# Mixer projections in three rounded passes, with their branch steps spread over them

## The reference

```python
proj = jnp.einsum("bsd,de->bse", x, w_in)          # 1024 -> 10264 columns
(a_in, gdn_qkv, gdn_beta_in, gdn_decay_in, gdn_gate_in,
 sb_qkv, gla_qkv, gla_lr, gla_gate_in, merge_in) = jnp.split(proj, offsets, axis=-1)
y_a = rg_lru(a_in, ...)                            # causal conv, two gates, scan
qkv = silu(causal_depthwise_conv(gdn_qkv, w))      # then l2-normalised q, k
beta, g = sigmoid(gdn_beta_in), -exp(a_log) * softplus(gdn_decay_in + bias)
y_b = gated_delta_rule(q, k, v, g, beta) ...
y_c = stick_breaking_attention(sb_qkv)
y_d = gla_chunked(gla_qkv, log_sigmoid(gla_lr @ w_gate_up + b) / 16) ...
merged = sum(sigmoid(merge_in[:, :, n]) * (y_n @ w_branch[n]) for n in range(4))
h = merged @ w_out
cos, sin = rope_tables(positions_2, 64)            # used by the second block
```

## Time and profile before

| | |
|---|---|
| median of 3 runs (lowest, highest) | 2191.77 us (2181.67, 2192.86) |
| the profiled execution: its time, its span | 2185.02 us, 2183.2 us |
| mean granted TensorE clock | 0.946 of full |
| busy: PE, DVE, ACT | 2065.7, 1189.5, 903.8 us |

### The profile page before, as it was taken

One profiled execution on the slowest core, in us unless ns is written; L12 is line 12 of the kernel. 1 busy time (PEld: TensorE's weight loads), 2 busy tenths in 40 slices (PEclk: granted clock), 3 DMA queues, 4 the chain that ended last, 5 costly groups with the idle time before them and its releaser, 6 DMA issues.

```text
span 2183.2 us, 29690 instructions
## 1 busy us (share of the span) xinstructions
PE 2065.7 (95%) x12013; PEld 1714.5 (79%) x12013; DVE 1189.5 (54%) x1686; ACT 903.8 (41%) x1300; POOL 60.7 (3%) x144
## 2 busy tenths in 40 slices
PE   8999999989989999998999987999999999879998
PEld 6777778787548888876999962489999999747998
DVE  2060353441269898898655646354565555455544
ACT  1232520211047777675433524443443435464333
POOL 5000000000000000000000000000000000000000
PEclk9999996987979999998999997999999999989999
DMA  7875250302579999996465579455555556403652
GB/s 239 282 262 176 94 174 20 103 14 97 199 323 348 342 351 333 336 350 251 157 198 184 188 307 373 140 173 190 174 194 189 175 173 211 137 25 112 214 189 97
DMA packets 207241, 441.81 MB, mean 202 GB/s; under 512 B 8108, under 2 KB 158732, under 8 KB 183584
## 3 DMA queue, kind: packets, MB, share of 16 engines
q1 hardware_dynamic: 201568, 424.70, 56.0%
q0 software_dynamic: 5568, 15.67, 2.1%
HBM read 439.14 MB, written 1.20 MB: 202 GB/s over the span
## 4 chain that ended last, share of the span: by engine, by line
PE 68%; DVE 6%; ACT 3%; DMA 2%; issue 1%; SPq 0%; ACTq 0%; DVEq 0%
PE P L679 67%; DMA ring<-in_ada_w 1%; ACT merged L1494 1%; DVE w_lo L2032 1%; DVE h L1985 1%; DVE xs L1985 1%; DVE xs L1978 0%; ACT pT L1494 0%; PE P L1206 0%; DMA ring<-in_w_up 0%; DVE w_lo L2427 0%; ACT st L1494 0%; ACT big L1494 0%; DMA ring<-in_w_gate 0%; PE P L1322 0%
## 5 line engine op out<-in xcount | busy, mean ns | idle before, releaser
L679 PE MATMUL P<-x_parts,w_hi 128*128 128x256 f32 x2560 | 458.2, 281 | 2.1 <-DVE w_lo L2032 2.1
L679 PEld LDWEIGHTS P<-x_parts,w_hi 128*128 128x128 f32 x2560 | 399.1, 189 | 8.9 <-DVE w_lo L2032 2.8
L2032 DVE TENSOR_TENSOR w_lo<-ring,w_hi 128x1024 fp32r<-128x1024 f32 x302 | 351.5, 1219 | 80.1 <-ACT w_hi L1526 79.9
L679 PE MATMUL P<-w_hi,x_parts 128*128 128x256 f32 (+2 forms) x1504 | 373.1, 335 | 2.2 <-DVE w_lo L2427 2.2
L679 PE MATMUL P<-x_parts,w_lo 128*128 128x256 f32 x1280 | 361.2, 282 | 0.0
L1526 ACT ACTIVATE w_hi<-ring 128x1024 fp32r<-128x1024 f32 x302 | 297.4, 1050 | 51.4 <-DMA ring<-in_ffn_w_down 48.5
L2427 DVE TENSOR_TENSOR w_lo<-ring,w_hi 128x1024 fp32r<-128x1024 f32 x240 | 281.1, 1221 | 32.5 <-ACT w_hi L1724 29.7
L679 PEld LDWEIGHTS P<-w_hi,x_parts 128*128 128x128 f32 x1504 | 260.9, 193 | 31.1 <-issue 3.3
L1724 ACT ACTIVATE w_hi<-ring 128x1024 fp32r<-128x1024 f32 x240 | 240.6, 1052 | 87.1 <-DMA ring<-in_w_down 31.0
L679 PE MATMUL P<-xT,ring 128*128 128x256 f32 x1152 | 267.4, 389 | 6.9 <-ACT xT L1494 3.1
L679 PEld LDWEIGHTS P<-xT,ring 128*128 128x128 f32 x1152 | 222.5, 195 | 53.6 <-issue 23.1
(11 more groups left out here) (439 smaller groups left out, 2035.8 us busy)
## 6 DMA issues: line engine op xcount, KB each, us to landing
ring<-in_ada_w SPq DMA_DIRECT2D x72, 1024.0 KB, 8.8
ring<-in_ffn_w_gate SPq DMA_DIRECT2D x44, 1024.0 KB, 5.5
ring<-in_ffn_w_up SPq DMA_DIRECT2D x44, 1024.0 KB, 7.9
ring<-in_ffn_w_down SPq DMA_DIRECT2D x44, 1024.0 KB, 4.9
ring<-in_w_in SPq DMA_DIRECT2D x40, 1024.0 KB, 7.4
ring<-in_w_gate SPq DMA_DIRECT2D x40, 1024.0 KB, 5.0
ring<-in_w_up SPq DMA_DIRECT2D x40, 1024.0 KB, 5.0
ring<-in_w_down SPq DMA_DIRECT2D x40, 1024.0 KB, 5.2
```

Of the source, the lines that this page charges most:

```text
L679: return pe.matmul(o, l, r, start=start, stop=stop, **kw)
L2032: dve.tensor_tensor(w_lo[:, slot, c:c + half], ring[:, slot, c:c + half], w_hi[:, slot, c:c + half].bitcast(F32), ALU.subtract).then_inc(s ...
```

## The change

P2 to P23 run in three float32r passes. `x` gets a high and a low part (`xm_hi`, over the place of `xs`, and `xm_lo`); the weights' high parts go to `wm_hi`, two units deep, over the place of `rowbc`. ACT's and DVE's halves of a unit's split are a step `split`, p, two units ahead: it stands behind P(p-2) (p = 3: behind `cols`) and ahead of the branch steps put there. `xs` is loaded a second time by POOL, after the last projection. The small products are one group of 40 rows in three passes, behind P2; a step `beta` transposes the 8 beta and decay rows back, behind P3. The `b_conv` and `a_conv` steps are cut into tiles and spread over P4 to P15, `a_mult` is cut in two, `b_silu` comes in three pieces. `b_norm` stands behind P18 (before: P19), `c_z` 0 behind P21 (before: P22). The 20 `ada` units stand behind P2 to P17. The `angles` and the sine go to merges 24 and 29. `x` is loaded in two halves at the start, ACT loads its table for the copies ahead of them, and the first two merges wait each for its own bank. The semaphores of the a, b and d branches are shared (`branch_act`, `branch_dve`), with the same waits.

```diff
     STEPS[k:k] = steps
 
 
-_put(("proj", "a", 1), [("cols",), ("small",), ("a_conv",)])
-_put(("proj", "b", 3), [("angles",)])
-_put(("proj", "b", 7), [("a_gates",)])
-_put(("proj", "c", 0), [("a_mult",)])
-_put(("proj", "c", 1), [("a_scan",)])
-_put(("proj", "c", 5), [("b_conv",)])
-_put(("proj", "d", 3), [("b_norm",)])
+PROJ = list(STEPS)
+WHOLE = 2
+
+
+_put(PROJ[1], [("cols",)])
+_put(PROJ[2], [("small",)])
+_put(PROJ[3], [("beta",)])
+_put(PROJ[4], [("a_conv", 0)])
+_put(PROJ[5], [("a_conv", 1), ("b_conv", 0)])
+_put(PROJ[6], [("b_conv", 1), ("b_conv", 2)])
+_put(PROJ[7], [("b_conv", 3), ("b_conv", 4)])
+_put(PROJ[8], [("b_conv", 5), ("b_conv", 6), ("b_silu", 0)])
+_put(PROJ[9], [("b_conv", 7), ("a_gates",)])
+_put(PROJ[10], [("b_conv", 8), ("b_silu", 1)])
+_put(PROJ[11], [("a_mult", 0)])
+_put(PROJ[12], [("a_mult", 1)])
+_put(PROJ[13], [("b_conv", 9), ("b_conv", 10)])
+_put(PROJ[14], [("a_scan",)])
+_put(PROJ[15], [("b_conv", 11)])
+_put(PROJ[16], [("b_silu", 2)])
+_put(PROJ[18], [("b_norm",)])
+for p in range(WHOLE, len(PROJ)):
+    _put(("cols",) if p == 3 else PROJ[p - 2], [("split", p)])
 for n in reversed(range(EARLY_ADA)):
-    _put([s for s in STEPS if s[0] == "proj"][2 + n * 17 // EARLY_ADA], [("ada", n)])
...
+_put(("split", 23), [("c_z", 0)])
 STEPS.append(_MERGE[0])
...
 
...
         w_lo = buf("w_lo", 128, R, UNIT, dt=F32R, ctx=m0)
         m0.close()
         ring = buf("ring", 128, R, UNIT)
+        m0 = ExitStack()
+        xm_hi = buf("xm_hi", 128, DT, S, dt=F32R, ctx=m0)
+        buf("xT_place", 128, DT, S, ctx=m0)
+        wm_hi = buf("wm_hi", 128, 2, UNIT, dt=F32R, ctx=m0)
+        m0.close()
         xs = buf("xs", 128, 2, D)
         m0 = ExitStack()
...
-            sp.dma_start(xs[:, :, :], A["x"][0].rearrange("(i p) d -> p i d", p=128)).then_inc(sem("x_here"), 16)
+            for i in range(2):
+                sp.dma_start(xs[:, i, :], A["x"][0][i * 128:i * 128 + 128, :]).then_inc(sem("x_rest" if i else "x_here"), 16)
             passed, after_unit = Counter(), []
             for n in range(len(loads)):
...
             store_quad(1, 0)
+            pool.wait_ge(sem("proj_out"), 2 * len(PROJ))
+            load(xs[:, :, :], A["x"][0].rearrange("(i p) d -> p i d", p=128), "ln_here")
             pool.wait_ge(sem("b_read"), 1)
...
-                return x
-
-            def cm_units(n):
-                for _ in range(n):
-                    w = take().rearrange("p (m n) -> p m n", n=256)
-                    for c in range(2):
-                        tile_cm(w, c * 128)
-
-            def tm_unit():
-                tiles_tm(take().rearrange("p (m n) -> p m n", n=256))
+
+            def split_unit(p, rows):
+
+                n = unit[0]
+                unit[0] += 1
+                lo_wait(pe, n)
+                w = [part.rearrange("p (m n) -> p m n", n=256) for part in (wm_hi[:, p % 2, :], w_lo[:, n % R, :])]
+                for k in range(2):
+                    bank, r = proj_bank(), slice(k * 128, k * 128 + 128)
...
+                        if rows:
+                            x = mm3(P[:, bank, 0:256], (xm_hi[:, d, r], xm_lo[:, d, r]), [part[:, d, :] for part in w],
+                                    start=d == 0, stop=d == DT - 1)
+                        else:
+                            x = mm3(P[:, bank, 0:S], [part[:, d, r] for part in w], (xm_hi[:, d, :], xm_lo[:, d, :]),
+                                    start=d == 0, stop=d == DT - 1)
+                    t.tell(x, "proj")
 
             def p_cols():
...
-                pe.wait_ge(sem("small_here"), 64)
-                for i in range(2):
-                    for d in range(DT):
-                        mm(P[:, 2, 8 * i:8 * i + 8], xT[:, d, i * 128:i * 128 + 128], wsm[:, d, 0:8],
-                           start=d == 0, stop=d == DT - 1)
+                t.see("xm")
+                t.see("xm")
                 for d in range(DT):
-                    x = mm(P[0:16, 3, 0:S], wsm[:, d, 8:24], xT[:, d, :], start=d == 0, stop=d == DT - 1)
+                    x = mm3(P[0:40, 3, 0:S], [wsm_parts[:, h, d, :] for h in range(2)], (xm_hi[:, d, :], xm_lo[:, d, :]),
+                            start=d == 0, stop=d == DT - 1)
                 t.tell(x, "small_psum")
 
+            def p_beta():
+                t.see("beta_rows")
+                for i in range(2):
+                    x = pe.transpose(P[:, 2, 8 * i:8 * i + 8], tmpm[32:40, i * 128:i * 128 + 128], ident[32:40, 32:40])
+                t.tell(x, "small_psum")
+
             def p_proj(which, u):
...
+                p = PROJ.index(("proj", which, u))
+                if p < WHOLE:
+                    whole_unit()
+                    return
+                split_unit(p, which in "cd" and u in (4, 5))
...
-                    pe.wait_ge(sem("proj_out"), t.sent["proj"])
+                if k < 2:
+                    pe.wait_ge(sem("proj_out"), t.sent["proj"] - 1 + k)
                 if d % 4 == 0:
...
+                    pe.wait_ge(sem("x_rest" if i else "x_here"), 16)
...
+                act.wait_ge(sem("small_here"), 64)
+                f(wsm_parts[:, 0, :, 0:32].rearrange("p d (e n) -> p d e n", e=2), wsm[:, :, 8:24].unsqueeze(2).to_broadcast([128, DT, 2, 16]), ACT.Copy)
+                f(wsm_parts[:, 0, :, 32:40], wsm[:, :, 0:8], ACT.Copy, "xm_hi")
 
...
+            def a_beta():
+                a.see("small_psum")
                 f(small[:, 16:24].rearrange("p (i k) -> p i k", k=4), P[:, 2, 0:16].rearrange("p (i k) -> p i k", k=8)[:, :, 0:4],
                   ACT.Sigmoid, "beta")
-                f(lrT[:, :], P[0:16, 3, 0:S], ACT.Copy)
                 a.see("sp_in")
                 f(small[:, 44:56], small[:, 44:56], ACT.Exp)
                 f(small[:, 8:12], small[:, 4:8], ACT.Exp, "beta")
+
+            def high_proj(p):
+
+                n = marks["proj"][p]
+                act.wait_ge(sem("unit%d" % (n % R)), 16 * (n // R + 1))
+                for c in (0, UNIT // 2):
+                    act.activation(wm_hi[:, p % 2, c:c + UNIT // 2], ring[:, n % R, c:c + UNIT // 2], ACT.Copy).then_inc(sem("w_hi"), 1)
 
             def a_proj(which, u):
...
+            def a_a_mult(half):
+                if half:
+                    return
+                a.see("branch_dve")
                 f(a_t[:, :, :], a_r[:, :, :], ACT.Tanh)
-                f(a_r[:, :, :], a_r[:, :, :], ACT.Exp, "a_act")
+                f(a_r[:, :, :], a_r[:, :, :], ACT.Exp, "branch_act")
...
-            def a_b_conv():
-                a.see("b_conv")
-                f(qkv[:, :, :], qkv[:, :, :], ACT.Silu)
-                f(nsq[:, :, :], qkv[:, 0:8, :], ACT.Square, "squares")
+                a.see("branch_dve")
+                f(a_t[:, :, :], a_t[:, :, :], ACT.Sqrt, "branch_act")
+
+            def a_b_silu(g):
+                a.see("b_conv", 4)
+                f(qkv[:, 4 * g:4 * g + 4, :], qkv[:, 4 * g:4 * g + 4, :], ACT.Silu)
+                if g == 2:
+                    f(nsq[:, :, :], qkv[:, 0:8, :], ACT.Square, "squares")
...
+            table(ACT.Copy)
             take_xT()
+            f(xm_hi[:, 4:8, :], xT[:, 4:8, :], ACT.Copy, "xm_hi")
...
+                v.see("xm_hi")
+                hi, lo = (wsm_parts[:, h, :, 0:32].rearrange("p d (e n) -> p d e n", e=2) for h in range(2))
+                tt(lo, wsm[:, :, 8:24].unsqueeze(2).to_broadcast([128, DT, 2, 16]), hi.bitcast(F32), ALU.subtract)
+                tt(wsm_parts[:, 1, :, 32:40], wsm[:, :, 0:8], wsm_parts[:, 0, :, 32:40].bitcast(F32), ALU.subtract, "xm")
...
+            def low_proj(p):
+
+                n = marks["proj"][p]
+                for q, c in enumerate((0, UNIT // 2)):
+                    dve.wait_ge(sem("w_hi"), 2 * split_no[n] + q + 1)
+                    dve.tensor_tensor(w_lo[:, n % R, c:c + UNIT // 2], ring[:, n % R, c:c + UNIT // 2],
+                                      wm_hi[:, p % 2, c:c + UNIT // 2].bitcast(F32), ALU.subtract).then_inc(sem("w_lo"), 1)
+
+            def v_a_conv(half):
                 dve.wait_ge(sem("proj_out"), 4)
-                for c in range(4):
+                for c in (2 * half, 2 * half + 1):
                     conv(a_x[:, c, :], a_pad, V_CONV_A, 4, c, cols[:, V_CONV_AB + c:V_CONV_AB + c + 1])
-                v.mark("a_x")
+                if half:
...
-            def v_a_mult():
-                v.see("a_act")
-
-                ts(nsq[:, 0:4, :], a_t[:, :, :], -1.0, 1.0, ALU.mult, ALU.add)
-                recip(nsq[:, 0:4, :], nsq[:, 0:4, :])
-                stt(a_t[:, :, :], a_t[:, :, :], -2.0, nsq[:, 0:4, :], ALU.mult, ALU.mult, "a_dve")
+                    ts(a_r[:, c, :], a_r[:, c, :], small[:, 12 + c:13 + c], name="branch_dve" if c == 3 else None)
+
+            def v_a_mult(half):
+                if half == 0:
+                    v.see("branch_act")
+                c = slice(2 * half, 2 * half + 2)
+
+                ts(nsq[:, c, :], a_t[:, c, :], -1.0, 1.0, ALU.mult, ALU.add)
```

(41 more changed lines are left out.)

73 lines of the change are left out of this document (31 added, 42 removed).

## The result

The changed kernel takes **2155.68 us** (median of 4 runs, 2151.81 to 2159.59), beside 2192.14 of the kernel before in the same session: a ratio of **0.9833** [0.981, 0.9856]. The forecast was 2155. Two later sessions gave 0.9835 [0.9814, 0.9856] and 0.985 [0.9825, 0.9875].

What follows compares the result with a forecast made beforehand. The stretch to the first merge was taken as bound by PE's own work. Terms -30.9 - 5.6 - 2.5 + 0.4 + 4.6 - 1.4 (merge idle) + 1.7 = -33.7 us gave 2155, range 2140 to 2176.

Steps and rivals of the forecast that it cites:

- two bases 7 us apart: Starting times for the forecast: the profiled execution, giving 2151.3 us, and the median 6.8 us above it, giving 2158.1.
- Three passes: P2 to P23: 18 units save 1.42 us and four save 1.34, -30.9 us in all (bounds -31.2 and -24.2).
- Small products: The small products as 24 float32r matmuls and two small transposes: 3.3 us instead of 8.91, -5.6 us (-6.0 to -2.7).
- The start: Before P0: earlier table load and `x` in halves, first unit's landing then counts, -2.5 us (-1.3 to -2.7).
- Splits and ring at almost nothing: From P2 on: splits hidden except small catches, +0.4 us (0 to +13); the weights' DMA transfers cost zero.
- late splits: Rival: splits about a microsecond late at each of P6 to P18, +13 us, 2168; chance 0.17.
- `c_z` one unit earlier: At P23: waits for a PSUM bank behind ACT's in-order `c_z` chain, +4.6 us (0 to +5.5).
- Low clock behind the wait: Behind P23's wait: PE's granted clock at its lower level, +1.7 us (0 to +1.7).
- the ring: Rival, P2 to P17: DMA stays at 284 GB/s, 133 us instead of 117, +16 us, 2171; chance 0.08.
- the cooling at every seam: Rival, P2 to P23: PE waits for `w_lo` and cools, 4.0 us a unit, +88 us, 2243; chance 0.04.
- The full quarter: Rival: a projection takes 0.75 of 7.10 us, 5.33, another -8 us, 2147; chance 0.02.
- At nothing: Claimed to cost zero: `angles`, `sines`, `x` again on POOL, `ada` re-spacing, `b_norm` earlier, shared semaphores.

Runs made afterwards that it cites:

- experiment 2: The changed kernel with all 24 projections in whole float32 and no splits, small products still in three passes: 2183.35 us, ratio 0.9969.
- experiment 7: The changed kernel with the start of before (`x` in one transfer, table loaded behind the transposes): 2161.21 us, one run.
- experiment 6: The changed kernel with the `ada` units in groups of two and three behind every second projection: 2161.84 us, one run.
- experiment 3: The changed kernel with ACT's exp and ln of `c_z` 0 moved behind P22's copies and `gate_d` copied plainly, its SiLU behind P23: 2154.52 us, ratio 0.9829.
- experiment 4: The changed kernel with `c_z` 0 behind P22, as in the kernel before: 2165.33 us, one run.
- experiment 8: The changed kernel and the kernel of experiment 3 run again in one call: 2158.57 us and 2156.08 us.
- experiment 1: The changed kernel run again without any edit: 2156.5 us, ratio 0.9835.
- experiment 5: The changed kernel with all twelve `b_conv` tiles in one lump behind P15 and the SiLU pieces behind P16: 2181.29 us, one run.
- experiment 9: The kernel of experiment 3 with P1 in three passes too: 2152.4 us, ratio 0.983.

## Why the prediction was right

The time was right to 1 us, and part of that is luck: three terms were off by over a microsecond and nearly cancel (-33.7 forecast, -33.0 measured to the first merge), and 2155 is the middle between two bases 7 us apart. Against the medians the gain was 36.5, 34.1 and 30.9 us in three comparisons.

- **Three passes**: right in kind (experiment 2), mis-sized, 26.4 for 30.9. The step that failed is "18 units save 1.42 and four save 1.34". It took 7.10 from the earlier trace rows, where the projection stands between `ada` pieces and pays 0.1 us at each edge, and 5.68 from the earlier trace rows, where the unit has no such edge. Like with like it is 7.10 to 5.90, or 6.91 to 5.68: 1.2 either way. The lower bound given, 0.3 us lost a unit at the seams, was the nearer end, with a wrong cause: it is no wait for DVE. On average a unit is 5.88 / 7.08 = 0.83 of before, and without the edges 5.68 / 6.91 = 0.82. That is further still from the three quarters that follow from the Trainium skill (FP8 and Floating Point Precision, TensorE Precision Notes); the trace does not agree with that figure as a ratio of times.
- **Small products**: -5.9 for -5.6. The pitch of 128 stationary columns held for 40: 24 matmuls in 2.83 us.
- **The start**: -2.2 for -2.5, with the releaser as forecast (experiment 7).
- **Splits and ring at almost nothing**: right. DVE is busy for 44.9 of 55 us in the densest part and no `w_lo` is late. P8's halves are done 2 us ahead and P14's 1.6, for 1.5 each in the prediction; DVE is busy for 80.4 of the 104.8 us from P3's to P17's end, for 87 of 102. The margin is thin: nine high halves wait for their landing, and experiment 6 shows both rivals, late splits and late landings, come true when the `ada` pieces are bunched. The cover is the single piece between projections.
- **`c_z` one unit earlier**: the mechanism was right and is shown from three sides (experiments 3, 4, 8). The size, 3.1 for 4.6, is off mainly by one table load that the new order saves (1.28): the step "2.75 + 7.6 + 0.4 + 0.4" took over the chain of the earlier trace rows with that load in it.
- **Low clock behind the wait**: +1.6 for +1.7; P23's window has 0.77. But the upper bound of 1.7 was too low: in two of six traces with this wait (experiments 1 and 5) it cost 2.7.
- **Clock at P0 and P1**: -1.7, not foreseen, and not the change's: it comes and goes between executions.
- **The rivals**: late splits (2168), the ring (2171) and the cooling at every seam (2243) did not come. PE's clock is 1.00 from 25 to 187 us. The Trainium skill (TensorE: Matmul & The Clock Gate, HAM oscillation) describes the loss of a kernel that waits for each operand; from P2 to the first merge it shows here behind P23's wait alone. The full quarter (2147) is refuted by the unit's 5.88.
- **At nothing** (angles, sines, `x` again, later `ada`): the merges take 333.2 us, 334.7 before; nothing of these edits is to be seen. They were not tried one by one.

## What to carry over

Take both sides of a difference from rows with the same neighbours: a projection between one-column pieces costs 0.2 us more than one among its own kind, in float32 as in three passes, and setting one with such edges against one without made the largest error here. When operands are prepared two units ahead by other engines, small pieces of other work between the units are the cover; the same pieces in groups cost 10 us. And the copy out of PSUM must not stand behind a chain with table loads, though removing such a wait (4.8 us in the trace) may give back half or more by the clock: time it, don't only read the trace.

## Of the hardware, not expected

- An `ada` piece (one stationary column) or a `c_z` product (64 rows) beside a product of 128 stationary columns costs PE 0.1 us at each edge, whatever the type: 0.30 to 0.32 us where 0.216 is the pitch in float32, 0.21 to 0.23 where 0.12 is. A change between float32 and float32r costs nothing where both have 128 columns (0.12 at 192.27, and experiment 9).
- A stretch at the lower clock need not begin behind a wait: the one around the wait of 1.17 us had begun some 10 us ahead of its end, with PE busy on small matmuls, and it ended 3.4 or 5.9 us behind it. Which of the two went with a shift of the work ahead.
- The first two projections took 13.9 to 17.0 us in different executions, with no wait in them, though the trace's granted clock reads 1.00 there in most. The trace has no record of the clock before 16.1 us in experiment 1 and none before 8.8 in the changed kernel's first, and a stretch without a record reads 1.00. In experiment 1 P0's matmuls start 0.43 us apart up to that first record and 0.22 from there on, so this is the lower clock.
